# Bias of the wide jobs added by VectorE and ScalarE, and a job's 32 further rows gathered as quarter rows

## What is computed

```python
hid = jnp.dot(xblk, w1[e]) + b1[e]
glu = jnp.minimum(hid[:, 0::2], SWIGLU_LIMIT)
lin = jnp.clip(hid[:, 1::2], -SWIGLU_LIMIT, SWIGLU_LIMIT)
act = glu * jax.nn.sigmoid(SWIGLU_ALPHA * glu) * (lin + 1.0)
return jnp.dot(act, w2[e]) + b2[e]
```

## Time and profile before

| what | value |
|---|---|
| runs | 2197.22, 2200.66, 2201.6 us |
| the profiled execution, its own time | 2203.66 us |
| its span | 2202.1 us |
| granted TensorE clock, mean | 0.974 |
| TensorE busy, of the span | 2050.6 us (93%) |
| VectorE busy | 1600.1 us (73%) |
| ScalarE busy | 1296.1 us (59%) |
| GpSimd busy | 423.2 us (19%) |
| DMA moved | 506.10 MB |

### The profile page before, as it was taken

The page is one execution under the profiler, slowest core; times in us unless marked ns, Lnnn a source line. Parts: engine busy times, 40 slices in busy tenths (PEclk is TensorE's granted clock), DMA queues, the critical chain, the costliest instruction groups (busy, mean ns, idle before and its releaser), DMA issues. The chain is left out here.

```text
span 2202.1 us, 40266 instructions
## 1 busy us (share of the span) xinstructions
PE 2050.6 (93%) x11606; PEld 1763.0 (80%) x11607; DVE 1600.1 (73%) x2206; ACT 1296.1 (59%) x1869; POOL 423.2 (19%) x478
## 2 busy tenths in 40 slices
PE   7999977778957999999999999999999999999994
PEld 6888867777846878889798897979898888979883
DVE  5342176985657677878878787888788797887876
ACT  5221245563436576766757667677667676675765
POOL 3100000220241131221213121132212131121311
PEclk9999989999978999999999999999999999999997
DMA  5221210004247897979889798899898797988978
GB/s 182 61 82 58 67 68 1 11 20 159 96 156 254 278 305 243 352 247 327 287 278 333 237 353 267 297 314 358 253 318 302 257 349 248 334 284 278 331 239 309
DMA packets 260913, 506.10 MB, mean 230 GB/s; under 512 B 34496, under 2 KB 35520, under 8 KB 260566
## 3 DMA queue, kind: packets, MB, share of 16 engines
q1 hardware_dynamic: 243064, 458.05, 60.5%
q0 software_dynamic: 17792, 47.33, 8.8%
q10 hardware_dynamic: 4, 0.02, 0.0%
HBM read 466.10 MB, written 39.22 MB: 229 GB/s over the span
## 5 line engine op out<-in xcount | busy, mean ns | idle before, releaser
L1820 DVE TENSOR_TENSOR wlo<-raw,whi 128x1024 fp32r<-128x1024 f32 x774 | 932.1, 1219 | 75.6 <-ACT whi L1296 67.7
L1296 ACT ACTIVATE whi<-raw 128x1024 fp32r<-128x1024 f32 x775 | 846.1, 1116 | 221.6 <-PE ps L981 162.8
L979 PE MATMUL ps<-xT,whi 128*128 128x320 f32 x1920 | 525.2, 350 | 5.6 <-DMA brow<-brow_d 5.0
L981 PE MATMUL ps<-xT,wlo 128*128 128x160 f32 x1920 | 456.4, 238 | 0.0
L979 PEld LDWEIGHTS ps<-xT,whi 128*128 128x128 f32 x1920 | 364.0, 190 | 10.0 <-issue 6.6
L981 PEld LDWEIGHTS ps<-xT,wlo 128*128 128x128 f32 x1920 | 369.8, 193 | 0.2
L2088 POOL DMA_INDIRECT acc_d<-y,icur x64 | 102.6, 1604 | 947.9 <-ACT y L1330 885.3
L621 PE MATMUL ps<-whi,xT 128*128 128x512 f32 x544 | 216.0, 397 | 0.0
L621 PE MATMUL ps<-whi,aT 128*128 128x512 f32 x512 | 213.1, 416 | 1.3
L623 PE MATMUL ps<-whi,xT 128*128 128x512 f32 x544 | 213.3, 392 | 0.0
L622 PE MATMUL ps<-wlo,xT 128*128 128x512 f32 x544 | 213.1, 392 | 0.0
(11 more groups left out here) (300 smaller groups left out, 3484.4 us busy)
## 6 DMA issues: line engine op xcount, KB each, us to landing
raw<-in_w SPq DMA_DIRECT2D x780, 512.0 KB, 7.4
raw<-in_w_in SPq DMA_DIRECT2D x16, 512.0 KB, 4.7
xs<-in_x SPq DMA_DIRECT2D x8, 512.0 KB, 10.5
raw<-in_w_out SPq DMA_DIRECT2D x8, 512.0 KB, 3.9
mix<-in_x SPq DMA_DIRECT2D x8, 512.0 KB, 4.2
acc_d<-mix SPq DMA_DIRECT2D x8, 512.0 KB, 5.0
h_d<-h SPq DMA_DIRECT2D x8, 512.0 KB, 2.6
mix<-acc_d SPq DMA_DIRECT2D x8, 512.0 KB, 7.5
```

The source lines that it names most:

```text
L979: pe.matmul(o2, wh[:, a, cols], xT2[:, :, k, 0:JOB_T], start=q == 0 and a == 0, stop=False, skip_group_check=True)
L981: m = pe.matmul(o, wl[:, a, cols], xT2[:, 0, k, 0:JOB_T], start=False, stop=q == QUARTERS - 1 and a == 1, skip_group_check=True)
L1296: act.activation(parted(slot(whis, s)), paired(raw_slot(s), s), ACT.Copy).then_inc(split_hi, 1)
L1820: dve.tensor_tensor(parted(slot(wlos, s)), paired(raw_slot(s), s), parted(slot(whis, s).bitcast(F32)), ALU.subtract).then_inc(split_lo, 1)
```

## The change

1. **Bias of wide jobs.** The 16 products of line 984 go. `b1` is loaded once more before the jobs, transposed by 16 small transposes into columns (`bcolT`, 1 added to the linear half), and for each job GpSimd copies its expert's columns into `bcur`. ScalarE adds the gate half as the bias of its sigmoid (two instructions of 160 columns in place of one of 320), VectorE the linear half by one more instruction for each of four units.
2. **`brow` for the next job** is loaded by GpSimd in `next_bias`, behind step 15 (its columns are copied there too), not by SyncE behind its last weight load.
3. **The fold** of the 32 further rows of a wide job moves from VectorE to GpSimd: ScalarE writes all 64 partitions into `y`, GpSimd copies the upper 32 and adds them, for unit 4 and for unit 5, and only then issues the first scatter.
4. **Quarter rows.** The 32 further rows are gathered as 128 quarter rows of 1 KB on 128 partitions (`xq`). `load_slots` issues five DMAs in place of three, GpSimd computes 4 x number + quarter by one more instruction, and one turn of two transposes stands in place of turns 2 and 3 of four each (`X_TURN_AT` ends with turn 2 behind step 21). A job then has ten transposes in place of 16.

```diff
-X_TURN_AT = {18: (0,), 19: (1,), 21: (2,), 22: (3,)}
+X_TURN_AT = {18: (0,), 19: (1,), 21: (2,)}
+X_TURNS = 3
...
+            sp.dma_start(b1r[:, :], b1[0]).then_inc(b1r_in, 16)
...
-                    wait(quarter_used, j * NS + 4 * (DENSE_UNITS + 4))
-                    wait(brow1_in, j * 16 + 16)
-                    sp.dma_start(brow[0:2, 0:2 * FF].bitcast(F32),
-                                 bias_part(en, slice(0, 2 * FF))).then_inc(brow1_in, 16)
...
+                rows = xg[:, 4 * r * P:4 * (r + 1) * P] if r < 2 else xq[:, :]
+                for k in range(4 if r < 2 else 2):
+                    m = pe.transpose(ps[:, 6 + r % 2, k * P:(k + 1) * P], rows[:, k * P:(k + 1) * P], ident[:, :])
...
-                        if q == 0:
-                            pe.matmul(o, brow[:, c * UNIT + 256 * odd + P * i:c * UNIT + 256 * odd + P * (i + 1)], ones2[:, 0:JOB_T],
-                                      start=False, stop=False, skip_group_check=True)
...
-                    act.activation(sigw[:, :, :], gsum[:, :, :], ACT.Gelu_apprx_sigmoid).then_inc(sig_set, 1)
+                    for i in range(2):
+                        m = act.activation(sigw[:, i, :], gsum[:, i, :], ACT.Gelu_apprx_sigmoid,
+                                           bias=bcur[:, 0, 2 * c + i:2 * c + i + 1])
+                    m.then_inc(sig_set, 1)
...
-                    act.wait_ge(y_set[1], j * 2 + c - 3)
-                    act.activation(yfold[:, c - 4, :], ps[HALF:2 * HALF, out_bank(2, c, 1), :], ACT.Copy,
-                                   scale=gcur[HALF:2 * HALF, 1:2]).then_inc(yfolded, 1)
+                    act.activation(y[0:2 * HALF, 1, (c - 4) * UNIT:(c - 3) * UNIT], ps[0:2 * HALF, out_bank(2, c, 1), :], ACT.Copy,
+                                   scale=gcur[0:2 * HALF, 1:2]).then_inc(yfolded, 1)
...
+                dve.tensor_tensor(lsum[:, :, :], lsum[:, :, :],
+                                  bcur[:, 1, 2 * c:2 * c + 2].unsqueeze(2).broadcast_to([P, 2, JOB_T]),
+                                  ALU.add).then_inc(lin_biased, 1)
...
-                for i in range(0, 2 * HALF, HALF):
+                for i in range(0, P, HALF):
                     pool.dma_start(tnext[i:i + HALF, 1, :],
                                    table_d[bass.ds(part * JOB_T + P, HALF), :]).then_inc(tnext_in, 16)
...
+                pool.tensor_scalar(inext[:, 1:2], tnext[:, 1, 0:1], 4.0, qcol[:, 0:1], ALU.mult, ALU.add).then_inc(tnext_cast, 1)
+                wait(tnext_cast, 3 * j + 2)
+                pool.indirect_dma_start(out=xg[:, :], out_offset=None, in_=h2_d,
+                                        in_offset=bass.IndirectOffsetOnAxis(ap=inext[:, 0:1], axis=0)).then_inc(gathered, 16)
+                pool.indirect_dma_start(out=xq[:, :], out_offset=None, in_=h2_d.rearrange("t (q n) -> (t q) n", q=4),
+                                        in_offset=bass.IndirectOffsetOnAxis(ap=inext[:, 1:2], axis=0)).then_inc(gathered, 16)
...
+            def y_fold(j, c):
+
+                wait(yfolded, j * 2 + c - 3)
+                cols = slice((c - 4) * UNIT, (c - 3) * UNIT)
+                pool.tensor_copy(yfold[:, c - 4, :], y[HALF:2 * HALF, 1, cols]).then_inc(low_moved, 1)
+                pool.wait_ge(low_moved, j * 2 + c - 3)
+                pool.tensor_tensor(y[0:HALF, 1, cols], y[0:HALF, 1, cols], yfold[:, c - 4, :], ALU.add).then_inc(y_set[1], 1)
+                pool.wait_ge(y_set[1], j * 2 + c - 1)
...
+                if blocks == 2:
+                    next_bias(j, e)
+                    y_fold(j, 4)
+                    y_fold(j, 5)
                 for b in ((0, 1) if blocks == 2 else (1, 0)):
```

More of the change, by code:

```diff
@@ L81 @@
 B_AV, B_HI, B_HG, B_OUT = 0, 128, 640, 1152
+BTILES = FF // P
 F32 = mybir.dt.float32
@@ L927, in _ @@
                       jobr[:, :, :].rearrange("p a b -> p (a b)"), start=True, stop=True).then_inc(job_sum, 1)
+            pe.wait_ge(b1r_in, 16)
+            for two in range(2):
+                for i in range(BTILES):
+                    cols = slice(2 * P * i + two, 2 * P * (i + 1) + two - 1, 2)
+                    m = pe.transpose(ps[:, 3, (two * BTILES + i) * NE:(two * BTILES + i + 1) * NE],
+                                     b1r[:, cols], ident[0:NE, 0:NE])
+            m.then_inc(bias_turned, 1)
             def x_turn(r):
[L932 to L935, removed]
+                rows = xg[:, 4 * r * P:4 * (r + 1) * P] if r < 2 else xq[:, :]
+                for k in range(4 if r < 2 else 2):
+                    m = pe.transpose(ps[:, 6 + r % 2, k * P:(k + 1) * P], rows[:, k * P:(k + 1) * P], ident[:, :])
                 m.then_inc(x_turned, 1)
@@ L940, in _ @@
             pe.wait_ge(gathered, 32)
-            for r in range(4):
-                if r >= 2:
-                    pe.wait_ge(xT_lo, r - 1)
+            for r in range(X_TURNS):
+                if r == 2:
+                    pe.wait_ge(xT_lo, 1)
                 x_turn(r)
@@ L1899, in job @@
                         (hidden if blocks == 1 else hidden_wide)(j, UNIT_END[s - 1])
-                    if blocks == 2 and UNIT_END.get(s - 1, 0) == 4:
-                        y_fold(j, 4)
                     jsplit(j, s + AHEAD)
@@ L2039, in _ @@
                     pool.wait_ge(brow_zero, 2)
-                    link(pool.memset(xg[:, 1, :], 0.0))
-                    link(pool.memset(tnext[:, 1, :], 0.0))
+                    pool.dma_start(brow[0:2, 0:2 * FF].bitcast(F32), bias_part(0, slice(0, 2 * FF))).then_inc(brow1_in, 16)
+                    for q in range(4):
+                        link(pool.memset(qcol[HALF * q:HALF * (q + 1), :], float(q)))
                 pool.wait_ge(pos_set, t + 1)
@@ L2059, in gather @@
             def gather(j):
-                wait(tnext_in, j * 48 + 48)
-                pool.tensor_copy(inext[:, :], tnext[:, :, 0]).then_inc(tnext_cast, 1)
-                wait(tnext_cast, 2 * j + 1)
-                for b in range(2):
-                    n = (P, HALF)[b]
-                    pool.indirect_dma_start(out=xg[0:n, b, :], out_offset=None, in_=h2_d,
-                                            in_offset=bass.IndirectOffsetOnAxis(ap=inext[0:n, b:b + 1], axis=0)
-                                            ).then_inc(gathered, 16)
+                wait(tnext_in, j * 80 + 80)
@@ new lines, in gather, with columns, next_bias @@
+                pool.indirect_dma_start(out=xq[:, :], out_offset=None, in_=h2_d.rearrange("t (q n) -> (t q) n", q=4),
+                                        in_offset=bass.IndirectOffsetOnAxis(ap=inext[:, 1:2], axis=0)).then_inc(gathered, 16)
+            def columns(e):
+                pool.tensor_copy(bcur[:, :, :], bcolT[:, :, :, e].rearrange("p a i o -> p a (i o)")).then_inc(bcur_set, 1)
+            def next_bias(j, e):
+                wait(quarter_used, j * NS + 4 * (DENSE_UNITS + 4))
+                wait(brow1_in, j * 16 + 16)
+                pool.dma_start(brow[0:2, 0:2 * FF].bitcast(F32), bias_part(e, slice(0, 2 * FF))).then_inc(brow1_in, 16)
+                wait(act_set, j * 4 + 4)
+                columns(bass.ds(e, 1))
+                wait(bcur_set, j + 2)
@@ L2107, in _ @@
             pool.wait_ge(y_zero, 1)
+            pool.wait_ge(bcolT_set, 1)
+            columns(slice(0, 1))
+            pool.wait_ge(bcur_set, 1)
             with pool.Fori(0, JOBS, 1) as j:
```

75 lines of the change are left out of this document (46 added, 29 removed).

## The result

The changed kernel takes 2177.65 us (median of four runs, 2171.12 to 2183.6) against 2199.3 for the kernel before: ratio 0.9892, 95% interval 0.9873 to 0.9911. It is 1.1% faster; 2222 was forecast, with the time on the slower side. The profiled execution took 2183.6 us with a span of 2181.8; the one of before had a span of 2202.1, so the two traces differ by 20.3 us.

The account below looks back on a forecast made before the run. TensorE was taken as the bound, with GpSimd's gather chain close behind. Against the profiled 2203.7 us, -39.5 - 5 + 1 + 49 + 16 = +21.5 gave 2225, as a median 2222; range 2180 to 2262.

Parts of the forecast that it names:

- TensorE's own work: On TensorE, bias products removed save 22 us and fewer turns of transposes 17.5, together 39.5 us.
- waits before turn 0: In narrow jobs behind wide ones TensorE waits for the later last gather: 49 us, from 28 to 91.
- clock: Behind TensorE waits of about 4 us the granted clock halves: 14 times 0 to 2.6 us, taken as 16.
- start, with `brow`: At the start, `brow` waits gone save 5 us, between 0 and 7; loads and transposes ahead of the jobs add 1.
- the delay D: On GpSimd's chain between the wide job's end and the narrow job's gathers: 5.4 us added, from 3.9 to 8.2.
- rival A: GpSimd's chain stays short, faster below a D of 5.0 us with no clock lost; 2185 or 2157 us; chance 0.28.
- The fold: On GpSimd ahead of the first scatter: copy and addition delay the chain 3.1 us, from 2.5 to 4.9.
- Two small DMAs and one instruction: On GpSimd ahead of the gathers: two DMAs in `load_slots` add 1.06 us, one more instruction 0.6 (0.28 to 1.3).
- The second gather: On GpSimd, 128 descriptors of rows in place of 32 add 0.65 us, from 0.1 to 0.9.
- hidden, 0 us: VectorE's four adds less two folds, +0.5 us in a wide job, are covered by idle time; without cover 7 us.
- rival C: VectorE becomes the bound in narrow jobs, TensorE waits for splits: 50 us, 2272 if both in full; chance 0.05.
- F: The forecast itself, 2205 to 2262 us, chance 0.59; a third has both fold instructions behind whole VectorE splits, 2248 us.

Follow-up runs that it names:

- bias_only: Changed kernel with the whole-row gather, three small DMAs and four turns of before put back; bias, `brow` and fold on GpSimd stay: 2168.68 us, ratio 0.9853.
- fold_vector: Changed kernel with the fold of the 32 further rows back on VectorE, all else as changed: 2152.3 us, ratio 0.9781.
- quarter_only: Kernel before with the quarter rows alone; bias products, `brow` by SyncE and fold on VectorE as before: 2188.11 us, ratio 0.9934.
- after_one_dma: Changed kernel with one DMA, its source repeated four times, in place of four DMAs of 32 partitions: 2169.78 us, ratio 0.9860.
- after_two_more: Changed kernel with two more small DMAs in `load_slots`, into a tile nobody reads: 2204.22 us, ratio 1.0010.
- experiment 6: Changed kernel without the wait between the row-number cast and the quarter-row instruction: 2167.67 us; the same edit on top of after_one_dma: 2161.79 us.
- experiment 4: Changed kernel with small DMAs issued early as in slots_early and the fold on VectorE as in the kernel before: 2147.32 us, ratio 0.9749.
- slots_early: Changed kernel with the five small DMAs of `load_slots` issued right behind the gathers of the job before, fold still on GpSimd: 2142.06 us, ratio 0.9734.
- slots_early_fold_vector: Changed kernel with both edits, small DMAs issued ahead of the scatter and the fold back on VectorE: 2147.32 us, ratio 0.9749.

## Why the prediction was wrong, step by step

The sum was +21.5 against the profiled execution, and the traces differ by -20.3. Its four terms:

| term | forecast | measured | from |
|---|---|---|---|
| TensorE's own work | -39.5 | -52.7 | 15 x 2.36, and 17 x 1.02 (37.36 less 36.34, jobs without a wait) |
| waits before turn 0 | +49 | +29.1 | the rows of the 14 waits |
| clock | +16 | +8.2 | five jobs of 1.65 |
| start, with `brow` | -4 | -5.4 | fourth job 9.8 sooner, less 4.4 of steady gain |

The measured terms add up to -20.8, for -20.3 in the spans. Two leftovers of about 3 us each cancel in that: turn 0 comes 31.8 us later in all where the idle time is 29.1, and some narrow jobs of before were longer than 37.36, 37.57 on average.

**The step that failed is the delay D, "3.1 + 1.06 + 0.6 + 0.65 = 5.4 us".** It was 4.1: the last gather is issued 4.62 later and lands 0.5 sooner. The rest of that calculation stands: with 4.1 the same formula, nine jobs with 1.35 to spare and five with 2.9, gives 9 x 2.75 + 5 x 1.2 = 31 us, and 29.1 were measured. It also stood in the text that the kernel is faster below a D of 5.0 with no clock lost, or below 3.9 with 16 us of clock lost; with the 8.2 that were lost this border is at 4.4, and D fell just on the other side of it. So it is the rival A, given 0.28, that came. Its time of 2185 had no lost clock and the same gain of TensorE as the forecast. D alone does not bring the forecast to the measured time either: the 20 us of waits take 2222 to 2202. The other 21 are the two terms below, TensorE's gain (13) and the clock (8). The parts of D:

- The fold: 3.1 estimated, and the first scatter is indeed 2.9 late (3.1 in bias_only). But the last gather is only 2.06 late (bias_only against before, and the changed kernel against fold_vector). Half a microsecond is gone at the start of the copies of the token numbers. Most of the rest is in them: before, the one of line 2072 was held up by a split and took 1.19 us, and now, where none meets it, it takes 0.38. I took a delay at the head of a chain for the delay at its end.
- Two small DMAs and one instruction: 1.66 estimated, 2.54 measured (quarter_only; 2.56 between bias_only and the changed kernel). The DMAs show 2.04 for four, so 1.0 as said; the rest, about 1.5, is the instruction, at the upper end of its 0.28 to 1.3 and beyond. after_one_dma warns not to take this split too literally, as an issue's time isn't paid in full.
- The second gather: +0.65 estimated, "from 0.1 to 0.9", and measured about -0.5. Its issue takes 0.1 longer at most, but it lands sooner, counted from the start of the issue: 6.4 against 6.9 us on average. The sum counted descriptors and left the landing at that of whole rows. The lower bound left out a gain, for no row that I had.

**The clock** was sized by two rows, 2.81 without loss and 3.81 with. In the changed kernel none of six waits of about 1.0 us lost it, four of seven of about 2.6 did and so did the one of 5.1, and in after_two_more all five of 3.7 to 3.8. Each of these cost some 1.65 us; the one of 3.50 us in quarter_only cost 2.2, at a granted clock of 0.50 over the next 5 us. Windows behind the two waits of 2.5 us shown above:

```profile
984.00:989.00 5.00, 5.00 (x28) 4.16 (x28) 3.83 (x5) 4.27 (x6) 0.00 (x0) 1.00 1.06 387
...
1674.80:1679.80 5.00, 5.00 (x20) 4.13 (x20) 2.34 (x3) 2.79 (x4) 0.00 (x0) 0.66 1.06 388
```

The levels, 1.2 and 2.4 GHz, are those of the earlier trace rows; what tells the two waits apart stays open.

**TensorE's gain** was 13 us short. A wide job gave 2.36 us for 2.12 forecast (1.76 of products, less the 0.3 for `y_set`, plus 0.66 of turns). Alone, bias_only gave 1.56 for the 1.46 of the products and quarter_only 0.79 for the turns: both were put a little low. A narrow job gave 1.02 and not 0.44. Of this 0.37 is the fold's leave from VectorE, "hidden, 0 us" in the text: there I looked at the wide job, where VectorE has room, and not at the narrow job behind it, where it has 0.13 us in 20 and carries the second fold. The rest, 0.2, is turn 2, which was to free nothing because its product waits for VectorE; in quarter_only, with the fold still on VectorE, the shortest narrow jobs are 36.7 us, already 0.6 shorter.

**What was right:** the place, the releaser and 14 of 15 jobs of the new wait; the first scatter 5 us behind the job's start; wide jobs about 2.2 us shorter; no wait for `brow` at the second job; no wait for VectorE's splits in its place, rival C, except for one of 3.19 us at the third job's start. The fold's additions took 1.29 us and its copies 0.60 or 1.22, within their bounds. The case in which each of the two instructions waits a whole split out, a third of F, did not come. By the rule of the Trainium skill that was weighed there (SBUF — State Buffer, Who interferes with whom) the two engines lock each other out; the trace agrees, with the 2.18 us split and the steps of experiment 6. But it works both ways: the fold, once in, makes the split wait (30 splits, 26 us, experiment 4), and no wait of TensorE shows that.

**A version that beats both:** slots_early, 2142.06 us, 2.7% below the kernel before.

## What to carry to other kernels

A chain with slack costs nothing up to a point and everything behind it. Price the edits of a change together against that point, and read from the trace how far every job stands from it: here two parts gained 34 and 14 us alone and 25 together. Where a chain of small instructions runs beside a busy engine that locks it out, as GpSimd's did here, its times lie on a grid; a delay is taken in whole steps or vanishes, so a sum of durations gives at best the mean delay. And before paying for such a chain, look whether its longest piece, here the landing of token numbers known a job ahead, must stand in it at all.

## What the runs showed of the hardware

- 128 rows of 1 KB gathered to 128 partitions landed 6.35 to 6.56 us behind the start of their issue (quarter_only, 6.41 on average), 32 rows of 4 KB 6.61 to 7.00 (bias_only, 6.84), with the DMA share at 1.05 in both. The bytes are the same, and the one with four times as many rows is the faster. It is not so everywhere: in slots_early_fold_vector, where its issue takes 1.90 us in place of 1.1, the gather of 128 rows landed at 6.71 to 7.37.
- One DMA for 128 partitions took 0.75 us to issue where four of 32 took 2.04, and GpSimd waited 4.8 to 6.4 us behind its end where it waited 4.6 to 5.3 behind the four. Of the 1.3 us, 0.95 reached the last gather.
- A GpSimd instruction of one column took 0.19 to 0.26 us where it met no split of VectorE, and where it met one until the end of it or of the instruction behind it, 2.38 at most (quarter_only). 0.09 ahead of a split it came through; 0.11 ahead, but upon VectorE's `glu`, it did not. VectorE's split took 2.18 in place of 1.22 where it came 0.2 us behind an addition on GpSimd.
- Behind a wait of TensorE of 2.5 to 2.6 us the granted clock fell in four jobs of seven and stayed at 1.00 in three (changed kernel); behind 0.96 to 1.06 us it stayed in all six, and behind 3.7 to 3.8 it fell in all five (after_two_more).
